# RWKV scan and output projection of a hybrid DiT layer: tile products of the output stage in the scan's tail, gates ahead of the averages, two places for the spreads, and waits for single results in place of three barriers

## The reference

```
# features
w_log = -softplus(-(w0 + tanh(lw) @ w2)) - 0.5;  decay = exp(-exp(w_log))
a = sigmoid(a0 + la @ a2);  gate = sigmoid(lg) @ g2
kk = l2_normalize(heads(k * k_k));  k_dir = k * (1 + (a - 1) * k_a)
# scan, forward and backward, chunked in the kernel
S_t = S_{t-1} (diag(w_t) - kk_t^T (a_t kk_t)) + v_t^T k_t;  y_t = S_t r_t
# output
y = y_forward + y_backward + bonus
out_rw = head_group_norm(y, ln[0], ln[1]) * gate        # mean and variance per head
mix = concat([out_dn, out_rw]) @ w_out;  h = h + g2 * mix
```

## Time and profile before

| | |
|---|---|
| median of 3 runs | 4044.11 us (4041.28 to 4049.51) |
| profiled execution, its own time | 4048.02 us |
| its span | 4046.3 us |
| TensorE, weight loads, VectorE, ScalarE, GpSimd busy | 94%, 83%, 55%, 36%, 19% |
| output stage, layer 0 / layer 1 | 59.06 us / 52.89 us |

### The profile page before, as it was taken

The page is one execution under the profiler, slowest core; times in us unless marked ns, Lnnn a source line. Parts: engine busy times, 40 slices in busy tenths (PEclk is TensorE's granted clock), DMA queues, the critical chain, the costliest instruction groups (busy, mean ns, idle before and its releaser), DMA issues. The chain is left out here.

```text
span 4046.3 us, 93176 instructions
## 1 busy us (share of the span) xinstructions
PE 3823.4 (94%) x40271; PEld 3339.7 (83%) x40271; DVE 2205.7 (55%) x3770; ACT 1453.4 (36%) x2510; POOL 757.2 (19%) x879
## 2 busy tenths in 40 slices
PE   7999999999988889999999999999999978889999
PEld 5899997878867767999998999987887857757887
DVE  4655556466464444755557555566565464444444
ACT  4322334343353333433234323343343253333222
POOL 1222210043023310222211222200232043300000
PEclk8999999999999999999999999999999989999999
DMA  6433332100200011333223333332000200032232
GB/s 213 126 118 106 104 106 70 47 3 2 81 5 4 5 70 42 112 95 93 84 75 112 108 104 104 110 104 58 22 2 21 66 2 4 4 110 81 86 112 65
DMA packets 409036, 287.20 MB, mean 71 GB/s; under 512 B 13438, under 2 KB 366180, under 8 KB 408164
## 3 DMA queue, kind: packets, MB, share of 16 engines
q1 hardware_dynamic: 408676, 281.86, 22.8%
HBM read 270.27 MB, written 11.53 MB: 70 GB/s over the span
## 5 line engine op out<-in xcount | busy, mean ns | idle before, releaser
L799 ACT ACTIVATE w_hi<-w_raw 128x512 fp32r<-128x512 f32 (+1 forms) x724 | 405.1, 612 | 649.0 <-POOL w_raw L783 348.0
L806 DVE TENSOR_TENSOR w_lo<-w_raw,w_hi 128x512 fp32r<-128x512 f32 (+1 forms) x724 | 484.2, 708 | 174.1 <-ACT w_hi L799 174.1
L914 PE MATMUL PS<-x_hi,w_hi 128*128 128x384 f32 x1680 | 562.4, 335 | 0.7 <-DVE hid_flat L1101 0.7
L914 PE MATMUL PS<-x_lo,w_hi 128*128 128x384 f32 x1680 | 561.3, 334 | 0.0
L914 PE MATMUL PS<-x_hi,w_lo 128*128 128x384 f32 x1680 | 561.2, 334 | 0.0
L1186 DVE SCALAR_TENSOR_TENSOR arena<-PS,mod,arena 128x256 f32<-128x256 f32 (+1 forms) x336 | 198.2, 631 | 331.6 <-PE PS L927 331.4
L1101 DVE TENSOR_TENSOR hid_flat<-hid_flat,PS 128x384 f32<-128x384 f32 (+1 forms) x454 | 245.6, 556 | 237.6 <-PE PS L914 153.6
L927 PE MATMUL PS<-hidden_hi,w_hi 128*128 128x256 f32 (+1 forms) x1232 | 342.0, 347 | 7.6 <-DVE hidden_lo L1153 5.7
L927 PE MATMUL PS<-hidden_hi,w_lo 128*128 128x256 f32 (+1 forms) x1232 | 337.0, 343 | 0.0
L927 PE MATMUL PS<-hidden_lo,w_hi 128*128 128x256 f32 (+1 forms) x1232 | 337.0, 343 | 0.0
L776 POOL TENSOR_TENSOR w_raw<-w_raw 128x512 f32<-128x512 f32 x60 | 85.3, 1421 | 1268.9 <-DMA w_raw<-in_ffn_w_dram 1184.4
(11 more groups left out here) (359 smaller groups left out, 7407.4 us busy)
## 6 DMA issues: line engine op xcount, KB each, us to landing
w_raw<-in_ffn_w_dram SPq DMA_DIRECT2D x512, 256.0 KB, 4.0
arena<-in_ada_w_dram SPq DMA_DIRECT2D x120, 512.0 KB, 5.8
arena<-in_w_in_dram SPq DMA_DIRECT2D x64, 512.0 KB, 3.9
arena<-in_ada_w_dram SPq DMA_DIRECT2D x6, 2048.0 KB, 14.2
arena<-in_w_out_dram SPq DMA_DIRECT2D x16, 512.0 KB, 4.5
h_save<-arena SPq DMA_DIRECT2D x16, 384.0 KB, 2.6
arena<-h_save SPq DMA_DIRECT2D x2, 3072.0 KB, 15.2
w_raw<-in_ffn_w_dram SPq DMA_DIRECT2D x32, 128.0 KB, 2.3
```

The source lines that it names most:

```text
L799: nc.scalar.activation(w_hi[:, high_place(n, what, j), 0:size], w_raw[:, load_of[what] % 2, place, 0:size], ACT.Copy).then_inc(w_high_read ...
L806: nc.vector.tensor_tensor(w_lo[:, b, place, 0:size], w_raw[:, b, place, 0:size], w_hi[:, high_place(n, what, j), 0:size].bitcast(F32), ALU ...
L914: mm = pe.matmul(PS[:, 4 * b + bank, 0:half], w[wo], x_split[xo][:, j, k, 0:half], start=(k == 0 and q == 0), stop=(k == KH - 1 and q == 2))
```

## The change

Three barriers go: the engines pass the ends of the projection, of the features and of the scan (`pass_phase`: drain and count, no wait), and wait for single results. GpSimd keeps its wait at the end of the projection.

- Features: Tanh moves to the end of ScalarE's projection; TensorE's `lora` waits for it, for the shifted inputs and for its PSUM banks. 27 hold products become 6.
- Scan: TensorE waits for KK, issues 14 hold products (8 before), and starts on the first chunk's first eight products of GpSimd, where all four engines' ends were awaited. The first turn also waits for the last bonus.
- Scan's tail: the two weight blocks and the saved half are copied once GpSimd's last chunk is made; ScalarE splits the weight blocks in the last step and the four DeltaNet blocks behind the last `move_u`, ahead of `move_out`. VectorE makes the low parts. TensorE's last step is new values, tiles(0), state on r, values on r, tiles(1) to tiles(3).
- Output stage: the four gates are made first, in two bank pairs in turn with the averages, and ScalarE moves each gate to `mix_rw`, where VectorE weighs it in place. Two spread places are used, and `spread(j + 2)` stands behind `tiles(NB + j)`.
- KD, KK, half of X_PAIRS and two masks move to other offsets, and the first two weight blocks and the low parts of the DeltaNet half have places of their own.

```diff
+            act.wait_ge(shift_step, 3 + 3 * (layer * RB + RB - 2))
+            nc.scalar.activation(lora_w, lora_w, ACT.Tanh).then_inc(lora_acted, 1)
...
         def act_feat(act, layer):
             sc = nc.scalar
-            sc.activation(lora_w, lora_w, ACT.Tanh).then_inc(lora_acted, 1)
...
             pe.wait_ge(lora_acted, layer + 1)
+            pe.wait_ge(shift_step, 3 + 3 * (layer * RB + RB - 1))
...
+                else:
+                    pe.wait_ge(rproj_moved, 3 + layer * RB + RB - 1 + d)
...
+            def last_step(c):
+                new_values(c)
+                pe_out_tiles(pe, layer, 0)
+                state_on_r(c, False)
+                values_on_r(c)
+                for k in range(1, NB):
+                    pe_out_tiles(pe, layer, k)
...
                     move_kb(d, 0)
+                    if d == RW_CHUNKS - 1:
+                        act_out_weights(act, layer, 0)
                     move_y(d, 3)
                     move_kb(d, 1)
+                    if d == RW_CHUNKS - 1:
+                        act_out_weights(act, layer, 1)
+                else:
+                    for k in range(NB):
+                        act_out_high(act, layer, k)
                 if c is not None:
                     move_out(c)
...
+            for t in range(2):
+                dve_out_weights(dve, layer, t)
+            for k in range(NB):
+                dve_out_low(dve, layer, k)
...
+            sp.wait_ge(rw_copied, (COPIES * RW_CHUNKS + ZEROED + WAYS) * (layer + 1))
             load(0)
             load(1)
...
+            dma_after(sp, start_of(layer, 7))
             for t in range(2, KT):
...
+            def take_gate(j):
+                bank_ = 4 + 2 * (j % 2)
+                act.wait_ge(go_summed, s0 + GATED[j])
+                sc.activation(mix_rw[:, j, 0:CTX], PS[:, bank_, 0:CTX], ACT.Copy)
+                sc.activation(mix_rw[:, j, CTX:T].rearrange("p (r c) -> p c r", r=GRID_H),
+                              PS[:, bank_ + 1, 0:SEQ].rearrange("p (c r) -> p c r", r=GRID_H), ACT.Copy).then_inc(go_act, 1)
...
+            gate(0)
+            pe.wait_ge(rw_out_moved, RW_CHUNKS * (layer + 1))
+            gate(1)
+            average(0)
+            average(1)
+            gate(2)
+            gate(3)
+            average(2)
+            average(3)
             pe.wait_ge(go_step, d0 + CENTERED[NB - 1])
...
+            spread(0)
+            spread(1)
             for j in range(NB):
+                pe_out_tiles(pe, layer, NB + j)
+                if j + 2 < NB:
+                    spread(j + 2)
...
             for j in range(NB):
+                scale(j)
+                weigh(j)
                 if j > 0:
-                    mix(NB + j - 1)
+                    dve_out_low(dve, layer, NB + j - 1)
...
                 pe_proj_rw(pe, layer)
-                pe_hold(pe, 6, 17)
-                end()
-                pe_hold(pe, 6, 10)
+                pass_phase(pe, "pe")
+                pe_hold(pe, 6, 6)
                 pe_feat(pe, layer)
-                end()
-                pe_hold(pe, 0, 8)
+                pass_phase(pe, "pe")
+                pe.wait_ge(kk_step, (1 + 2 * NB) * (layer + 1))
+                pe_hold(pe, 6, 14)
                 pe_rw(pe, layer)
-                end()
+                pass_phase(pe, "pe")
                 pe_out(pe, layer, segs_of(layer))
```

More of the change, by code:

```diff
@@ L82, in build @@
             m_split = [m_hi, placed(placing, "mix_lo", [P, KT, T], F32R)]
+        with ExitStack() as placing:
+            placed(placing, "below_mix_dn_lo", [P, 18432])
+            m_lo_dn = placed(placing, "mix_dn_lo", [P, NB, T], F32R)
         with ExitStack() as placing:
@@ L2627, in turn_x @@
                     pe.wait_ge(x0_ready, n0 + d + 1)
+                    if d == 0:
+                        pe.wait_ge(fe_dve, bonus_taken(layer, NB - 1))
                 else:
@@ L2768, in pe_rw @@
             for c, d in rw_steps():
-                step(c, d)
+                if d is not None:
+                    step(c, d)
+            last_step(RW_CHUNKS - 1)
         def act_rw(act, layer):
@@ L2988, in act_out @@
+            for j in range(NB):
+                square(j)
+            act.wait_ge(go_summed, s0 + 12)
             sc.activation(go_rows, RSTD[0:8, :], ACT.Sqrt, scale=1.0 / 64, bias=eps[0:8, 1:2]).then_inc(go_act, 1)
-            mix(2)
-            mix(3)
             act.wait_ge(go_step, d0 + 13)
@@ L3180, in _ @@
                 sp_proj_rw(sp, layer)
-                dma_after(sp, start_of(layer, 7))
                 sp_out(sp, layer)
@@ L3202, in _ @@
                 pool_feat(pool, layer)
-                end()
+                pass_phase(pool, "pool")
                 pool_rw(pool, layer)
@@ L3270, in _ @@
                 act_proj_rw(act, layer)
-                end()
+                pass_phase(act, "act")
                 act_feat(act, layer)
-                end()
+                pass_phase(act, "act")
                 act_rw(act, layer)
-                end()
+                pass_phase(act, "act")
                 act_out(act, layer, segs_of(layer))
@@ L3302, in _ @@
                 dve_proj_rw(dve, layer)
-                end()
+                pass_phase(dve, "dve")
                 dve_feat(dve, layer)
-                end()
+                pass_phase(dve, "dve")
                 dve_rw(dve, layer)
-                end()
+                pass_phase(dve, "dve")
+                dve.wait_ge(rw_out_moved, RW_CHUNKS * (layer + 1))
                 dve_out(dve, layer, segs_of(layer))
```

198 lines of the change are left out of this document (106 added, 92 removed).

## The result

The changed kernel takes 4058.0 us (median of 5 runs, 4050.9 to 4062.0), the kernel before beside it 4041.3 us (median of 5, 4033.2 to 4049.5). The ratio is 1.0037, 95% interval 1.0025 to 1.0049: **slower by 15 us (10 to 20)**, where 4035.9 was forecast and 4023 to 4046 was the range. The profiled execution is the shortest of its five, 4050.93 us for a span of 4049.2, so the two traces differ by 2.9 us in their spans alone. What each part did has to be read stage by stage, and the sum from the timed runs.

What follows compares the result with a forecast made beforehand. TensorE, busy for 94% of the span, was taken as the bound, with time to be had only in its waits or lower clock. Starts -14.8, output stage -3.6 and clock +10.2 made -8.2 us: 4044.1 to 4035.9, range 4023 to 4046.

Steps and rivals of the forecast that it cites:

- Starts: Features and scan start without barriers: first level product 7.4 us earlier (1.8 from the features), 14.8 us gained in two layers.
- Rival E: Scan's start: the 28 hold halves run at the lower clock level, 4.9 us a layer lost, 4045.7; chance 0.08.
- End of the scan: Block 0's tiles stand ahead of the scan's last two groups, so VectorE's adds start 3.9 us late in layer 0.
- Copies: Scan's last step: splitting two weight blocks there was taken at 0, with 2.1 us as the other bound.
- rival D: Scan's last steps: TensorE's instructions come late beside the copies, up to 5 us a layer, 4045.9; chance 0.10.
- Output stage before the clock: Output stage: head loses 3.5 us in layer 0, tail gains it back; net gains 1.4 and 2.2, together 3.6 us.
- The clock: Output stage's late tiles: one clock fall of 1.7 us for each of three long waits in both layers, 10.2 us lost.
- rival B: Output stage: every burst behind a long wait runs slow to its end, 20.0 us in all, 4045.7; chance 0.10.

Runs made afterwards that it cites:

- e1_starts: The kernel before with only the change's edits to the start of the features and of the scan; 0.9975 of the kernel before, 10 us faster (5 to 15).
- e4_holds: The changed kernel with hold products in its waits, 9 ahead of the early tiles and 18, 13, 13 ahead of the late ones; 1.0009 of the kernel before.
- e8_reordered: The changed kernel with tiles out of the scan, mixer output and residual stream copied behind it, spreads early, tiles between and behind them; 0.9919 of the kernel before.
- e6_copies_alone: The kernel before with only the copies of mixer output and residual stream (4.5 MB) moved ahead of the scan's last step; 1.0037 of the kernel before, 15 us slower.
- e9_filled: e8_reordered with tiles of blocks 0 and 1 further ahead and ScalarE's four high parts spread around the square root; 0.9925 of the kernel before, median 4010.3 us.

## Why the prediction was wrong

The forecast was -8.2 us, the result +15 (10 to 20). Step by step:

- **Starts: right.** 7.5 us of the first layer's start against 7.4, holds at 0.12 us, full clock; the second layer gained 5.1 in this trace and 6.8 in `e1_starts`. In timed runs the half alone brought 10 (5 to 15) against 14.8. Rival E did not happen.
- **End of the scan: the mechanism right, the size short.** The early tile stood ahead of the scan's own result as said. I priced it at 3.9 us a layer, with tiles at full clock; the tail grew by 5.6 and 4.4, because TensorE had idled 2.52 us and the burst ran at half; with holds ahead of it (`e4_holds`) the tail grew by 4.2 and 3.6. I had charged the clock only in the late turns.
- **Copies: the step that failed.** The sum prices the scan's last step at 0: I let the split of the weights start early at no cost, which holds (`e8_reordered` has it and takes 28.3 and 28.8 us), and put the copies' effect into rival D at 0.10. It is the largest single term: 6.0 and 5.2 us in the last step, in part idle time and in part the clock behind it, and 9 to 21 us when tried alone. D's price of up to 5 us a layer was about right, its chance was not. The waits at issue were the warning: they showed a supply that was late without any copies beside it. The Trainium skill says in "Runtime: NRT & Kernel Launch", "Instruction fetch mechanics", that the supply is mostly hidden. By it `e6_copies_alone` would be level with the kernel before; the trace disagrees, with waits of 4.75 and 2.85 us.
- **Output stage before the clock: nearly right.** From the adds to the first spread 28.6 us against 27.7 forecast.
- **The clock: right in kind, too small.** I counted one fall of 1.7 us for each of three waits, 5.1 a layer. In layer 0 two bursts ran at 0.50 from end to end and the third for 5.5 us, and the two spreads behind the first ones ran at 0.79 and 0.59: 1.9 + 1.9 + 2.8 for tiles and 1.1 for the spreads, 7.7. The like sum is some 6 in layer 1. I took the price from a burst that had recovered in its middle after a wait of 2.5 us, and did not ask whether longer waits are followed by longer falls. That is rival B, in part. The Trainium skill says in "TensorE: Matmul & The Clock Gate", section on HAM oscillation, that bursts with waits between them can start cold each time; the three bursts that start at 0.50 agree, and so do the 7 us that holds brought back.
- **The sum.** Put right, from the two traces: starts -12.6, last step +11.2, tail +10.0, output stage +5.7, together +14.3, inside the interval of the timed runs; the *scan* column, -11.0 in this pair by chance, is what hid it in the spans. The forecast had -14.8 for the starts, nothing for the last step and +6.6 for tail and output stage together (10.2 - 3.6), where the traces have +15.7. So of the 22.5 us between the two sums, 11.2 are the copies, 9.1 the tail and the output stage with their clock, and 2.2 the starts. B and D, held for alternatives at 0.10 each, happened at once, B in part. Alone, either would have left the time about level with before (4045.7 and 4045.9 against 4044.1). By the prices of the forecast both together make 4035.9 + 9.8 + 10 = 4055.7, 11.6 over before, which is inside what was measured. In the forecast's range there was no case with two of them.

## What to carry to other kernels

When a step is moved ahead, price its copies by what they run beside: a burst of megabytes next to a stretch of many small instructions can stall the engine that runs them, and with it those that wait for its results, even if nobody waits for the data. When two engines serve each other in turns, move the groups that feed the slower one ahead of the bursts that wait for it, and fill what is left of the waits with products that are due anyway; here a wait of several us on TensorE was paid twice, in the wait and in the clock behind it. And rivals that don't exclude each other need a case in which they come together.

## What the runs showed of the hardware

- TensorE stopped inside a group of equal, ready products for up to 4.75 us while copies of 4.5 MB were under way, and VectorE and ScalarE waited for its results. Beside 1 MB the longest such waits were 2.70 and 2.98 us (layer 1 of `e8_reordered` and `e9_filled`, last steps of 28.8 and 29.4 us, 27.4 before).
- In small matmuls, TensorE's waits at issue stood 252 to 256 matmuls and weight loads apart, or a multiple of it, in all of 999 distances of 13 traces, with copies and without.
- Behind waits of 4.83 and 3.65 us the granted clock stood at 0.50, the lower level, through whole bursts of 3.95 us, and at 0.79 and 0.59 over the spreads behind them; with 36 hold halves ahead of the first burst it stood at 1.00.
- The same scan, in 26 stretches of 13 traces, took from 216.6 to 227.4 us. In a single trace, an edit to this program worth less than 5 us a layer is seen only in its own stage.
